# Weights and row buffers moved from 16 to 32 columns (64 to 128 bytes) off the 256-byte lines of the moving operands

## The chip, the cores and the metric

The kernel runs on one core of a Trainium2 chip, all in float32. The metric is the device time of one execution in microseconds (us); three runs of the kernel before took 1356.17, 1356.43 and 1363.1 us. PE is the matrix engine, PEld its weight loads, DVE the vector engine, ACT the scalar engine, POOL and SP the two others.

## The reference, cut to what matters

256 tokens of width 1024 go through two transformer blocks, batch 1, one layer each.

```python
# block 1
h = rmsnorm(x, g1) * (1 + scale1) + shift1
proj = h @ w_in                                  # 1024 x 6976, split into 12 parts
ya = gla(gq, gk, gv, gr, glow) @ w_branch_a      # chunked gated linear attention
yb = sparse_attention(dq, dkv, iq, ik, iw) @ w_branch_b   # 64 keys kept for each query
x = x + gate1 * ((sigmoid(za) * ya + sigmoid(zb) * yb) @ w_out)
h2 = rmsnorm(x, g2) * (1 + scale2) + shift2
q = h2 @ peer_w_q                                # top 16 of 16384 experts, for 8 heads
a = gelu(h2 . u[idx]) * gate                     # 128 rows of u and of v for each token
x = rmsnorm(x + gate2 * sum(a * v[idx]))
# block 2
z = rmsnorm(x) @ w_in_2                          # gates, a 31-tap and a 3-tap causal convolution
x = x + (g_a * (silu(ln(conv(a))) @ w_a_out) + g_b * (s @ w_b_out)) @ w_o
u = rmsnorm(x) @ w_up_2                          # 1024 x 5632
x = x + (gelu(conv(u[:, :2816])) * u[:, 2816:]) @ w_down
x = rmsnorm(x + sigmoid(rmsnorm(x) @ w_ple_gate) * (p @ w_ple))
```

## The kernel before, in words

**Products in three passes.** Activations lie transposed in the on-chip memory: channels on the 128 partitions, the 256 tokens as columns. A float32 weight chunk is split into a high part (ACT copies it to the faster float32 format, line 1310, `hi`) and a low part (DVE subtracts, line 1917, `lo`, written over the raw chunk); the activations are split in the same way. A block of 128 output channels is then the sum over eight slices k of three matmuls, each with its own 128x128 weight load and 256 moving columns:

```python
pe.matmul(out, hi[:, k, c0:c0 + m], x_hi[:, k, 0:n], ...)   # line 754
pe.matmul(out, lo[:, k, c0:c0 + m], x_hi[:, k, 0:n], ...)   # line 755
pe.matmul(out, hi[:, k, c0:c0 + m], x_lo[:, k, 0:n], ...)   # line 756
```

Lines 794 to 796 (token-major products of `gv`, where the activations are the loaded side and the weights the moving one) and 1224 to 1226 (the down product) are the same three passes. A few products run once over whole float32 (line 746).

**Stages, in order of time.** To about 36 us PE forms norms and the first query products. From 36 to 303 us it works through the projections, attentions and output products of block 1, with weights in `ring`. From 303 to 367 us come the expert queries ("pq"), with activations `x2_hi`, `x2_lo` whose rows have 258 columns. From about 385 to 960 us the expert rows are gathered: POOL issues indirect DMAs of 8 KB per partition into 16 row buffers (`rows`, line 661), DVE forms the dot products (line 2335), ACT builds diagonal matrices `diag` (line 1582), and PE adds the scaled rows in plain float32 (line 1090). From 974 us on block 2 runs from 2 MB chunks in three raw slots and three `w_hi` slots; the up and down products take from 1154 to 1337 us. The order of the work on PE is written out by hand; a product waits by semaphores for its chunk and its output bank.

**Places in the partition.** Columns below are float32 columns, 4 bytes. The tensors are laid out by hand in one long stretch; `LINE` is 64 columns (256 bytes). All split activations (`n_hi`, `n_lo`, `g_`, `d_`, `m_`, `c_`, `h_`, `f_`, the first row of `x2_`) begin a whole number of lines from each other, and so does each slice k but in `x2_`, where each row is 258 columns and slice k so lies 2k columns on. The constant `ASIDE` (16 columns) sets the following that many columns past such a line: the ring (`a_ring`, with `e_raw`, `e_hi`, `e_lo`, `w_hi`, `pq_ring`), the raw slots and `w_lo` (`a_raw`), the first `hi` chunk, `pq_row`, the 16 row buffers, `diag`, the expert sums `pacc`, the score buffers `s_all`, and a few buffers behind the raw slots (`sT`, `scb`, `zg`, `scc`, `gelu2`, `otok`). Padding of `LINE - ASIDE` brings what follows back to a line. Chunks and their column blocks inside are whole multiples of 128 columns, so every weight of a three-pass matmul of one kind begins at the same place in its line.

Of the kernel before, what the change touches and what calls it, by code (L numbers as in the profile page):

```python
# [223 lines left out]
def two_blocks(nc, w, out):  # L224
    with ExitStack() as ctx:
# [29 lines left out]
        stat = sb("stat", [P, 2, T])  # L255

        SIZE = 28352
        LINE, ASIDE = 64, 16

        def overlay(*tensors):  # L260

# [2550 lines left out]
```

## Time and profile before

| what | us |
|---|---|
| median of three runs | 1356.43 |
| the profiled execution's own time | 1367.78 |
| its span in the trace | 1366.1 |
| PE busy | 1219.6 |
| PEld busy (overlaps PE) | 913.7 |
| DVE busy | 1065.1 |
| ACT busy | 612.5 |
| POOL busy | 285.8 |

A matmul's busy time runs from its start to its modelled end, and those of neighbours overlap: what a matmul takes of the engine is the distance from its start to the next one's. In a row of groups the mean ns of one is the length from start to end; a window's row counts the matmuls whose busy time touches the window. The idle time before a group is what PE stood still. Times in the trace's views are from the span's start.

### The profile page before, as it was taken

How to read it: one execution, taken by the hardware profiler on the slowest of the kernel's cores; microseconds unless marked ns; L12 is line 12 of the kernel's file. 1: busy time of each engine (PE TensorE's matmuls, PEld its weight loads, DVE VectorE, ACT ScalarE, POOL GpSimd, SP SyncE). 2: the span in 40 equal slices, each digit the busy share in tenths (PEclk: the TensorE clock that was granted, in tenths of full speed). 3: DMA queues.
4: the chain of work that ended last, by engine and by line, in shares of the span. 5: the costliest groups of instructions: out<-in, count | busy, mean ns of one | idle time of the engine just before them, and what ended most of it. 6: DMA issues, size and time to landing. Idle time of an engine off the chain costs nothing. (4 is left out here: it accounts for less than half of the span.)

```text
span 1366.1 us, 19459 instructions
## 1 busy us (share of the span) xinstructions
PE 1219.6 (89%) x6934; PEld 913.7 (67%) x6934; DVE 1065.1 (78%) x2167; ACT 612.5 (45%) x1267; POOL 285.8 (21%) x278
## 2 busy tenths in 40 slices
PE   8999999999997777777877777778999999999998
PEld 6999999999843232322322323223699999999998
DVE  7897678887997777777766777776799968989566
ACT  4666555655433333332333333323652356544345
POOL 1010000003374444434444443442000000000000
PEclk9999999999999999999999999999999999999999
DMA  9966446665999999999999999999744345554461
GB/s 390 375 223 257 175 176 226 246 217 225 353 425 428 427 427 428 427 428 427 426 428 427 427 428 427 428 427 426 286 157 173 130 169 188 179 187 170 165 226 44
DMA packets 55200, 416.64 MB, mean 305 GB/s; under 512 B 6081, under 2 KB 6721, under 8 KB 8658
## 3 DMA queue, kind: packets, MB, share of 16 engines
q0 software_dynamic: 36864, 268.45, 46.8%
q1 hardware_dynamic: 17792, 146.51, 29.1%
q8 instruction: 50, 0.82, 0.2%
q10 hardware_dynamic: 466, 0.63, 0.1%
q14 instruction: 28, 0.23, 0.0%
HBM read 414.52 MB, written 1.05 MB: 304 GB/s over the span
## 5 line engine op out<-in xcount | busy, mean ns | idle before, releaser
L1090 PE MATMUL ps<-arena 128*128 128x512 f32 x512 | 235.2, 603 | 66.0 <-ACT arena L1582 65.7
L1090 PE MATMUL ps<-ring,arena 128*128 128x512 f32 x440 | 210.2, 628 | 45.1 <-ACT arena L1582 44.5
L2335 DVE CUSTOM_DVE_ANT_0 arena<-arena 128x1024 f32<-128x1024 f32 x128 | 151.5, 1222 | 102.6 <-DMA arena<-in_experts,rowid 99.9
L1090 PEld LDWEIGHTS ps<-arena 128*128 128x128 f32 x512 | 92.5, 189 | 205.7 <-ACT arena L1582 110.9
L661 POOL DMA_INDIRECT arena<-in_experts,rowid x128 | 127.4, 996 | 354.1 <-DVE rowid L2262 183.5
L1090 PEld LDWEIGHTS ps<-ring,arena 128*128 128x128 f32 x440 | 85.2, 199 | 167.6 <-issue 91.6
L755 PE MATMUL ps<-h_hi,w_lo 128*128 128x256 f32 x700 | 195.7, 280 | 0.0
L1575 ACT ACTIVATE arena<-arena 128x2 f32<-128x2 f32 x126 | 25.6, 203 | 369.2 <-DVE arena L2335 369.0
L754 PE MATMUL ps<-h_hi,w_hi 128*128 128x256 f32 x672 | 189.5, 282 | 0.6 <-DVE w_lo L1917 0.4
L756 PE MATMUL ps<-h_lo,w_hi 128*128 128x256 f32 x672 | 187.9, 280 | 0.0
L2335 DVE CUSTOM_DVE_ANT_0 ring<-ring,arena 128x1024 f32<-128x1024 f32 x112 | 133.3, 1222 | 30.9 <-DMA ring<-in_experts,rowid 21.3
L661 POOL DMA_INDIRECT ring<-in_experts,rowid x112 | 129.7, 1158 | 130.9 <-PE ps L1090 86.3
L1917 DVE TENSOR_TENSOR w_lo<-arena,w_hi 128x4096 fp32r<-128x4096 f32 (+1 forms) x30 | 122.1, 4068 | 34.2 <-ACT w_hi L1310 33.6
L1310 ACT ACTIVATE w_hi<-arena 128x4096 fp32r<-128x4096 f32 (+1 forms) x30 | 100.2, 3341 | 74.1 <-DMA arena<-in_up_w 29.2
L755 PEld LDWEIGHTS ps<-h_hi,w_lo 128*128 128x128 f32 x700 | 131.7, 188 | 0.2
L754 PEld LDWEIGHTS ps<-h_hi,w_hi 128*128 128x128 f32 x672 | 127.7, 190 | 1.7 <-DVE w_lo L1917 1.3
L756 PEld LDWEIGHTS ps<-h_lo,w_hi 128*128 128x128 f32 x672 | 126.3, 188 | 0.0
L754 PE MATMUL ps<-n_hi,e_hi 128*128 128x256 f32 (+1 forms) x352 | 101.4, 288 | 0.2 <-issue 0.2
L755 PE MATMUL ps<-n_hi,e_lo 128*128 128x256 f32 (+1 forms) x352 | 98.0, 278 | 0.0
L756 PE MATMUL ps<-n_lo,e_hi 128*128 128x256 f32 (+1 forms) x352 | 98.0, 278 | 0.0
L1917 DVE TENSOR_TENSOR e_lo<-ring,e_hi 128x2048 fp32r<-128x2048 f32 (+1 forms) x38 | 86.3, 2271 | 12.5 <-ACT e_hi L1310 11.9
L1582 ACT ACTIVATE arena<-ident,arena 128x128 f32<-128x128 f32 x252 | 85.4, 386 | 0.0
(423 smaller groups left out, 2559.5 us busy)
## 6 DMA issues: line engine op xcount, KB each, us to landing
ring<-in_early_w SPq DMA_DIRECT2D x43, 1024.0 KB, 5.0
arena<-in_ada_w SPq DMA_DIRECT2D x24, 1024.0 KB, 8.7
arena<-in_up_w SPq DMA_DIRECT2D x11, 2048.0 KB, 7.9
arena<-in_z_w SPq DMA_DIRECT2D x8, 2048.0 KB, 8.0
arena<-in_down_w SPq DMA_DIRECT2D x8, 1408.0 KB, 6.0
arena<-in_o_w SPq DMA_DIRECT2D x2, 2048.0 KB, 8.4
arena<-in_early_w SPq DMA_DIRECT2D x3, 1024.0 KB, 6.5
arena<-in_experts,rowid POOLq DMA_INDIRECT x128
```

Of the source, the lines that this page charges most:

```text
L661: pool.indirect_dma_start(out=rows[j], out_offset=None, in_=w["experts"], in_offset=bass.IndirectOffsetOnAxis(ap=rowid[:, even, j:j + 1], ...
L754: pe.matmul(out, hi[:, k, c0:c0 + m], x_hi[:, k, 0:n], start=k == 0, stop=False, skip_group_check=True)
L755: pe.matmul(out, lo[:, k, c0:c0 + m], x_hi[:, k, 0:n], start=False, stop=False, skip_group_check=True)
L756: return pe.matmul(out, hi[:, k, c0:c0 + m], x_lo[:, k, 0:n], start=False, stop=k == KD - 1, skip_group_check=True)
L1090: mm = pe.matmul(BK[4 + 2 * t + b], diag[:, j, :], rows[j][:, D + b * 512:D + (b + 1) * 512], start=first and j == 0, stop=last and j == ( ...
L1310: act.activation(hi, whole, ACT.Copy).then_inc(S("w_hi"), 1)
L1575: act.activation(gel[:, even, two], dots[:, even, two], ACT.Gelu).then_inc(S("act_head"), 1)
L1582: act.activation(diag[:, j, :], ident[:, :], ACT.Copy, scale=amul[:, even, j:j + 1]).then_inc(S("diag"), 1)
L1917: v.tensor_tensor(lo, whole, hi.bitcast(F32), ALU.subtract).then_inc(S("w_lo"), 1)
L2335: v.tensor_tensor_reduce(out=u, in0=u, in1=h2tok[:, t, :], scale=1.0, scalar=0.0, op0=ALU.mult, op1=ALU.add, accum_out=dots[:, even, j:j + ...
```

## The change

One constant of the placement goes from 16 to 32 columns, 64 to 128 bytes:

```diff
         SIZE = 28352
-        LINE, ASIDE = 64, 16
+        LINE, ASIDE = 64, 32
```

Everything named above that stands `ASIDE` past a line moves on by 16 columns; what stands on a line stays where it was, and the total size is the same, since each step aside is paired with padding of `LINE - ASIDE`. No instruction, wait, DMA or size changes, and none changes its order. The distance from moving operand to weights goes from 16 to 32 columns in the three-pass products (for slice k of `x2_` from 16 - 2k to 32 - 2k; for lines 794 to 796, where weights move and activations are loaded, the other way round). `diag` and the row buffers move together, and so do raw chunk, `hi` and `lo`.

## Rows read from the trace of the kernel before

**Rows 1.** The page's first part: busy us, share of the span, instructions.
```profile
PE 1219.6 (89%) x6934; PEld 913.7 (67%) x6934; DVE 1065.1 (78%) x2167; ACT 612.5 (45%) x1267; POOL 285.8 (21%) x278
```

**Rows 2.** The page's second part: granted PE clock in tenths, 40 slices.
```profile
PEclk9999999999999999999999999999999999999999
```

**Rows 3.** Windows: stretch, length, PE, PEld, DVE, ACT, POOL busy, clock, DMA share, GB/s.
```profile
385.00:900.00 515.00, 400.07 (x858) 159.00 (x856) 382.45 (x988) 173.84 (x584) 227.10 (x216) 0.98 1.01 427
...
1020.00:1080.00 60.00, 60.00 (x438) 57.48 (x438) 59.06 (x114) 19.59 (x18) 0.00 (x0) 1.00 0.42 151
...
1200.00:1260.00 60.00, 60.00 (x512) 60.00 (x511) 54.06 (x81) 29.38 (x27) 0.00 (x0) 1.00 0.46 165
```

**Rows 4.** Who waited for whom on PE, 385 to 974 us: us, times, longest.
```profile
PE ps L1090 <- ACT arena L1582: 128.2, 91, 2.5
```

**Rows 5.** The same view, 1158 to 1341 us.
```profile
PE ps L754 <- DVE w_lo L1917: 0.2, 1, 0.2
```

**Rows 6.** The page's costliest groups: busy us, mean ns, idle before.
```profile
L755 PE MATMUL ps<-h_hi,w_lo 128*128 128x256 f32 x700 | 195.7, 280 | 0.0
...
L755 PEld LDWEIGHTS ps<-h_hi,w_lo 128*128 128x128 f32 x700 | 131.7, 188 | 0.2
```

**Rows 7.** Timeline of PE near 1200 us: start, length; nine matmuls.
```profile
1199.74 0.28 PE L755 MATMUL ps<-h_hi,w_lo 128*128 128x256 f32 x1
...
1200.68 0.28 PE L754 MATMUL ps<-h_hi,w_hi 128*128 128x256 f32 x1
```

**Rows 8.** The same near 1343 us; ten matmuls.
```profile
1342.75 0.28 PE L756 MATMUL ps<-h_lo,w_hi 128*128 128x256 f32 x1
...
1343.77 0.28 PE L756 MATMUL ps<-h_lo,w_hi 128*128 128x256 f32 x1
```

**Rows 9.** Groups by shape, 1200 to 1260 us, then 238 to 300 us.
```profile
L754 PE MATMUL ps<-h_hi,w_hi 128*128 128x256 f32 x170 | 47.8, 281 | 0.0
...
L755 PE MATMUL ps<-d_hi,e_lo 128*128 128x256 f32 x64 | 18.0, 281 | 0.0
```

**Rows 10.** Groups by shape: 90 to 100, 106 to 122, 1045 to 1060 us.
```profile
L755 PE MATMUL ps<-n_hi,e_lo 128*128 128x256 f32 x30 | 8.3, 276 | 0.0
...
L795 PE MATMUL ps<-e_lo,n_hi 128*128 128x256 f32 x48 | 13.2, 276 | 0.0
...
L754 PE MATMUL ps<-h_hi,w_hi 128*128 128x256 f32 x45 | 12.4, 276 | 0.0
```

**Rows 11.** Windows of PE alone: stretch, length, busy (count), clock, DMA share, GB/s.
```profile
85.00:103.00 18.00, 18.00 (x162) 1.00 0.57 192
...
236.00:300.00 64.00, 64.00 (x546) 1.00 0.65 236
303.00:333.00 30.00, 30.00 (x253) 1.00 0.49 176
...
1013.00:1033.00 20.00, 20.00 (x172) 1.00 0.55 211
1044.00:1063.00 19.00, 19.00 (x170) 1.00 0.31 111
...
1199.00:1271.00 72.00, 72.00 (x614) 1.00 0.44 160
1273.00:1335.00 62.00, 62.00 (x529) 1.00 0.57 207
```

**Rows 12.** Timeline of PE: a wait at 1158 us, other work at 1341 us.
```profile
1158.12 0.39 PE L754 MATMUL ps<-h_hi,w_hi 128*128 128x256 f32 x1 [0.22 <-DVE w_lo L1917]
...
1340.96 1.03 PE L1205 MATMUL ps<-sq,ones 128*128 128x256 f32 x4
1341.64 0.47 PE L754 MATMUL ps<-h_hi,w_hi 128*128 128x256 f32 x1
```

**Rows 13.** Groups by shape, 303 to 333 us: the 258-column rows.
```profile
L754 PE MATMUL ps<-x_hi,pq_row 128*128 128x258 f32 x48 | 13.9, 289 | 0.0
L755 PE MATMUL ps<-x_hi,pq_row 128*128 128x258 f32 x48 | 13.6, 283 | 0.0
```

**Rows 14.** DMA in 40 slices from 0 to 36 us: GB/s.
```profile
GB/s 0 5 155 355 437 419 428 437 392 437 428 419 437 437 437 391 401 437 437 419 437 437 419 428 391 410 337 428 437 401 419 437 396 423 442 459 410 419 428 410
```

## The prediction

> **What bounds the kernel now.** I read the engines' shares first: PE is busy 89% of the span [rows 1] and its clock is granted at the upper level, 2.4 GHz, nearly throughout [rows 2]. Then the windows, to see which stage has which limit. From 385 to 900 us the DMA engines are full, share 1.01 at 427 GB/s, while PE is busy 400 of 515 us and DVE 382 [rows 3]; PE waits 128 us in all for the diagonals [rows 4], which hang on the gathered rows. In this stage PE's own pace is worth nothing. In the two-block ends it is all: from 1200 to 1260 us PE is busy 60.00 of 60 us beside DVE's 54.06 [rows 3], and in the 183 us from 1158 to 1341 it waited once, for 0.2 us [rows 5]. So a nanosecond more or less per three-pass matmul there is a nanosecond of the kernel's time, until DVE is full.
>
> The reader is next to look at the pace, and the mean length of a group hides it: the costliest such group has 280 ns over 700 matmuls [rows 6]. The starts tell it. Near 1200 us eight steps take 1200.68 - 1199.74 = 0.94 us, 117.5 ns each [rows 7]; near 1343 us nine steps take 1.02 us, 113.3 ns each [rows 8]. Same instructions, same places of both operands, same clock, no wait. The length of a matmul goes with it, 281 ns in the slow rhythm [rows 9] and 276 in the quick one [rows 10], so that a row of groups shows at a glance which rhythm a stretch had. The windows confirm the sizes over many: 614 matmuls in 72 us, less about 2.4 that merely overlap the window's ends (281/117.7), make 117.7 ns; 162 in 18 us, less 2.4, make 112.8, which with the timeline's 113.3 I round to 113.3 [rows 11]. The difference taken is 4.4 ns.
>
> Each rhythm holds once it is there. It changes only where the stream is broken: by plain float32 products, as at 1341 us, after which it was quick, or by a wait, as at 1158 us, after which it stayed slow [rows 12]. Following the lengths through the trace I find slow some 118 us before 303 us (236 to 300 us is the longest piece) and some 249 us after 974 us, of which 183 are the up and down products in one piece; quick some 83 us before 303 (85 to 123 us the longest) and some 77 us after 974 (989 to 1009, 1044 to 1063, 1136 to 1154, 1343 to 1352) [rows 11]. That is 367 us of slow and 160 us of quick rhythm, about 3114 and 1412 matmuls.
>
> **The change part by part.** It adds, removes and moves no instruction, so every term is a change of pace or nothing.
>
> Three-pass products: their weights stand 16 columns from the moving operands' place, and will stand 32. What that does to the pace no row shows, since every such product of before, in both rhythms, has 16. The bounds come from the two rhythms and from one more row. If all slow stretches ran quick: 3114 x 4.4 ns = 13.7 us less (9.3 after 974 us, 4.4 before 303 us). If all quick ones ran slow: 1412 x 4.4 = 6.2 us more. The third row is the expert queries, whose slices stand at 16, 14, ... 2 columns' distance and at starts that aren't multiples of 4 columns: there the pace is neither, since 303 to 333 us hold 253 matmuls of which the 192 of three passes, with lengths of 283 to 289 ns [rows 13], take by the starts about 120.6 ns each. Such a pace everywhere would cost 3114 x 2.9 + 1412 x 7.3 = 19.3 us. So the bounds are -13.7 and +19.3 us.
>
> Which value I take: both rhythms stand at one and the same distance, so it isn't the distance alone that decides but the relative time of load and stream after each break. A new distance shifts the address phase of the two, hence at least throws the dice anew for every stretch. By the breaks of before, rather more than half fall into the slow rhythm (of twenty single blocks between 133 and 230 us 13 were slow; of nine long stretches after 974 us five). With 55% slow, 2490 of 4526 matmuls are slow instead of 3114: 624 x 4.4 = 2.7 us less. The draw is coarse, because the up and down products are one piece: they alone are worth 1550 x 4.4 = 6.8 us.
>
> The Trainium skill speaks against any effect at all. Its page SBUF — State Buffer, section "SBUF: two separate sides", has it that PE has ports of its own and never waits on anyone, and TensorE: Matmul & The Clock Gate, section "What happens when you issue a matmul", that the moving operand and the weight load have independent read ports, so that loading doesn't steal from the running matmul. By that rule the time would stay 1356.4; the two rhythms and the expert queries' 120.6 ns [rows 7, 8, 13] show that the pace of a stream with unchanged work does vary, and in the queries with the operands' places.
>
> Expert queries (303 to 367 us): distances go from 16-2k to 32-2k columns, about 380 matmuls. Taken as unchanged; the bounds are 380 x (113.3 - 120.6) = 2.8 us less and, mirrored, 2.8 us more.
>
> Row buffers: the gathers' landing places move by 64 bytes, from 16 to 32 columns past a line. Buffers on a line itself took 437 GB/s in the slices of the first 36 us [rows 14], those at 16 columns 427 with another kind of DMA [rows 3]. Taken at nothing; the bound is the distance of these two rows, 2.3% of 575 us, 13 us either way, which I hold for very unlikely as 64-byte multiples served both. `diag` and rows move together, so line 1090 keeps its distance, and its pace lies under the DMA anyway [rows 3, 4]. DVE's dot product reads one operand on a line and one aside: if it became slower, DVE has 132 us to spare in 515 [rows 3]. Raw, `hi` and `lo` move together, so lines 1310 and 1917 keep theirs.
>
> If PE gets quicker, DVE is late next: from 1020 to 1080 us it is already busy 59.06 of 60 us [rows 3], so gains there may be lost; 54.06 in 60 would be 54.06 in 57.7 between 1200 and 1260, still under.
>
> The sum: -2.7 us on the profiled execution's 1367.78 (span 1366.1 and 1.7 around it). That execution lies 11.35 us over the median of the runs, and the slow and quick shares of the others aren't shown; I apply the difference to the median: 1356.4 - 2.7 = 1353.7.
>
> **The rivals.**
> Quick everywhere. At 32 columns load and stream no longer meet at a bad phase, and each restart falls into the 113.3 ns rhythm. For it: a quick rhythm exists as a stable one at 16, and both 16 and, with roles exchanged, -16 hold it [rows 10]; 32 is the farthest place in a 64-column line. Against it: nothing shows that the phase counts in 64 columns. Its time: all of 9.3 us after 974, about half of 4.4 before 303, where chains through ACT and DVE also count: 11.5 less, 1344.9.
>
> Slow everywhere: 6.2 more, 1362.6. For it: the slow one already holds two thirds.
>
> A worse rhythm, the rival on the other side. Place: the three-pass stream, most of all 1154 to 1341 us, where nothing covers it [rows 5]. Mechanism: at the new distance the weight load meets the moving stream at a phase that costs more in every matmul, as in the expert queries, 120.6 ns or above. It decides from a mean pace of 118.5 ns: with 4526 matmuls at a mean of 116.4 now, 1.5 ns more is the 6.8 us of half a per cent. At 120.6 the time is 1375.7. Against it: the queries have odd starts in the line too, which the change makes nowhere new.
>
> No effect: the pace depends on the place within 64 bytes or less, and timing is unchanged to the nanosecond: 1356.4. This is what the skill's rule says; for it, that both rhythms occur at one distance.
>
> **How the numbers follow.** Within half a per cent (6.8 us) is what a measurement here can't tell from no change. Dice thrown anew 0.37 (0.09 of it faster, where the long stretch turns quick and little turns slow; 0.27 same; 0.01 slower); quick everywhere 0.24, faster; slow everywhere 0.10 (0.08 same, 0.02 slower); no effect 0.09, same; a worse rhythm 0.20, slower. So faster 0.33, same 0.44, slower 0.23. The likeliest gives 1353.7, its own range 1345 to 1361. Quick everywhere reaches down to 1342.7; of the worse rhythm I take in the nearer half, to 1372: range 1343 to 1372.
>
> **What would show it.** In the trace after: the group lengths by stretch (276, 281, or something else), and starts near 1200 us at 113.3, 117.7 or another distance. Dice: both lengths again, in other stretches. Quick everywhere: 276 throughout and PE idle time before line 754 growing as DVE becomes late. Worse: lengths over 282 in the up products. No effect: the same stretches with the same lengths. The stage from 385 to 960 us should keep its 427 GB/s; if its length changes by over 3 us, my zero for the row buffers was wrong. A third stable pace, or a change in stages without three-pass products, would make the prediction wrong in kind.

## The result, and the profile after

The changed kernel takes 1384.09 us in the median (1382.11 to 1384.97, four runs) against 1358.11 us (1356.17 to 1363.1, four runs) before: 1.0189 times as long, with a 95% interval of 1.0169 to 1.0208. That is 26 us slower, 12 us beyond the slow end of the predicted range. The profiled execution took 1384.97 us, with a span of 1383.2.

The windows of the kernel after, in the stretches of [rows 3] and [rows 11] (columns as in rows 3 for the first two; PE alone, as in rows 11, for the others):

```profile
400.00:900.00 500.00, 379.43 (x814) 148.79 (x813) 367.53 (x955) 166.45 (x555) 204.52 (x204) 0.99 1.01 422
1200.00:1260.00 60.00, 60.00 (x502) 60.00 (x501) 53.62 (x74) 26.57 (x25) 0.00 (x0) 1.00 0.51 186
...
236.00:300.00 64.00, 64.00 (x542) 1.00 0.66 241
...
1199.00:1271.00 72.00, 72.00 (x602) 1.00 0.49 181
```

Two things stand there. From 1199 to 1271 us PE is as full as before and gets through 602 matmuls where it did 614 [rows 11]. And while the expert rows are gathered, the DMA engines are as full as before, share 1.01, and move 422 GB/s where they moved 427 ([rows 3]; from 400 to 900 us it is 427 as well).

The groups by shape from 1200 to 1260 us, and PE's timeline there, two starts that lie fifteen matmuls apart:

```profile
L755 PE MATMUL ps<-h_hi,w_lo 128*128 128x256 f32 x168 | 47.7, 284 | 0.0
L756 PE MATMUL ps<-h_lo,w_hi 128*128 128x256 f32 x167 | 47.6, 285 | 0.0
L754 PE MATMUL ps<-h_hi,w_hi 128*128 128x256 f32 x167 | 46.9, 281 | 0.0
```

```profile
1219.82 0.28 PE L754 MATMUL ps<-h_hi,w_hi 128*128 128x256 f32 x1
...
1221.62 0.28 PE L754 MATMUL ps<-h_hi,w_hi 128*128 128x256 f32 x1
```

The lengths are neither 276 nor 281 ns throughout but 281, 284 and 285 [rows 9, 10], and the starts are 1.80 us / 15 = 120.0 ns apart. By the distances between starts, the trace after has two paces: 120.0 ns from 1170 to 1356 us, from 1053 to 1074 and from 127 to 159, and 118.6 ns nearly everywhere else. The quick rhythm of 113.3 ns is gone.

The page's row of GB/s in 40 slices shows the gathers at the new rate from slice 12 to 28; the granted clock is as in [rows 2]:

```profile
GB/s 388 373 215 238 189 157 234 237 218 230 355 423 420 423 421 422 422 422 421 421 421 421 421 422 422 422 422 422 298 142 170 140 170 177 182 183 164 162 221 36
```

### The profile page after: what moved, and what is told of

It reads as the page before. It is cut to its first block, busy times and chain, and to the rows that moved or that the text cites. A ratio compares the mean times of both kernels' runs of the same rounds, so it can differ in the third digit from the quotient of the medians.

```text
span 1383.2 us, 19459 instructions
## 1 busy us (share of the span) xinstructions
PE 1229.8 (89%) x6934; PEld 922.6 (67%) x6934; DVE 1065.1 (77%) x2167; ACT 612.8 (44%) x1267; POOL 274.8 (20%) x278
## 4 chain that ended last, share of the span: by engine, by line
PE 35%; DMA 30%; DVE 4%; issue 3%; ACT 2%; POOL 1%; DVEq 0%; ACTq 0%; POOLq 0%
DMA ring<-in_experts,rowid 30%; PE ps L1090 7%; PE ps L756 7%; PE ps L755 7%; PE ps L754 6%; PE ps L746 2%; PE ps L1226 2%; PE ps L1225 2%; PE ps L1224 2%; DVE ring L2335 1%; DVE h_rows L2335 1%; PE ps L1179 0%; ACT arena L1578 0%; ACT arena L1582 0%; POOL arena L661 0%
## 5 line engine op out<-in xcount | busy, mean ns | idle before, releaser
L661 POOL DMA_INDIRECT ring<-in_experts,rowid x112 | 118.4, 1057 | 141.3 <-PE ps L1090 103.9
```

The source lines that it names most:

```text
L661: pool.indirect_dma_start(out=rows[j], out_offset=None, in_=w["experts"], in_offset=bass.IndirectOffsetOnAxis(ap=rowid[:, even, j:j + 1], ...
```

## The experiments

The theory formed on this trace, A: two causes that have nothing to do with each other. The pace of the three-pass matmuls follows the **distance** between weights and moving operands in a 256-byte line; the time of a landing packet follows the **absolute place** of its destination. Its rivals: B, the absolute place of the weights decides both; C, the distance decides both. (By the addresses that the build assigns, the arena, which is the kernel's one long stretch, begins 41920 bytes into the partition, 192 past a multiple of 256. So before, weights and row buffers lay on multiples of 256 and after 64 past them. No trace shows this start. Were it another, each "past a multiple of 256" below would be past the place that the row buffers of before have in their line; the steps of 64 bytes between the kernels would stand. DMA records of the gathers' 8 KB packets, between 400 and 880 us and without the few over 340 ns, have a mean of 309.0 ns before, nearly all exactly 309, and of 313.6 after, mostly 312, some 319.)

**Each cause alone.** `e1_base64` keeps the distance and moves the whole layout; `e2_aside128_land0` has the new distance and the old absolute places of weights and row buffers. In both, 64 columns were taken out of a reserve so that the layout still fits.

```diff
-        sb("to_line", [P, 8])
+        sb("to_line", [P, 24])        # e1; e2: [P, 56], and ASIDE = 32
-        SIZE = 28352
+        SIZE = 28288
-        at[0] += LINE - 8 + ASIDE
+        at[0] += ASIDE - 8
```

> Distance of weights and moving operands as before (64 bytes), but the whole layout moved on by 64 bytes, so that weights and row buffers lie at the same absolute places in a 256-byte line as after the change (64 past a multiple of 256). Theory A (two causes: the pace of the three-pass matmuls follows the distance, the landing of DMA packets follows the absolute place): paces of 113.3 and 117.8 ns only, packets of the gathers at 312 to 319 ns as after the change, gather stage some 6.9 us longer than before: about 1365. Theory B (the absolute place of the weights decides both): paces of 118.6 and 120.0 as after, about 1384. Theory C (the distance decides both): as before, 1358.

> Distance of 128 bytes as after the change, but the base moved so that weights and row buffers lie on multiples of 256 bytes, as before. Theory A: paces of 118.6 and 120.0 ns, packets back at 309 ns, gather stage as before: 1384 - 7 = 1377. Theory B: paces of 113.3 and 117.8, all as before: 1358. Theory C: as after, 1384.

The ratio of the kernel after is to the four runs of before beside it (1358.11), the others' to the nine of the first row.

| kernel | distance, place of weights and rows (bytes past 256) | us, median | ratio to before (95%) | paces, ns | gather packets, mean ns |
|---|---|---|---|---|---|
| before | 64, 0 | 1356.99 (9 runs) | | 113.3 and 117.8 | 309.0 |
| after | 128, 64 | 1384.09 | 1.0189 (1.0169 to 1.0208) | 118.6 and 120.0 | 313.6 |
| e1 | 64, 64 | 1365.29 | 1.0059 (1.0042 to 1.0076) | 113.3 and 117.8 | 313.6 |
| e2 | 128, 0 | 1374.71 | 1.0123 (1.0095 to 1.0152) | 118.6 and 120.0 | 309.0 |
| e4 | 0, 192 | 1385.9 | 1.0207 (1.018 to 1.0234) | 120.0 | 313.7 |
| e5 | 192, 128 | 1375.89 | 1.0134 (1.0107 to 1.0161) | 117.8, two short stretches at 113.3 | 313.6 |

Windows of e1, then of e2 (columns as in rows 3):

```profile
400.00:900.00 500.00, 379.40 (x809) 148.43 (x808) 363.66 (x939) 167.52 (x559) 204.10 (x204) 0.98 1.01 422
1200.00:1260.00 60.00, 60.00 (x532) 60.00 (x531) 55.74 (x79) 30.22 (x28) 0.00 (x0) 1.00 0.49 178
```

```profile
400.00:900.00 500.00, 389.10 (x826) 153.89 (x824) 370.42 (x956) 168.78 (x564) 212.75 (x207) 0.97 1.01 427
1200.00:1260.00 60.00, 60.00 (x502) 60.00 (x501) 52.44 (x71) 26.89 (x27) 0.00 (x0) 1.00 0.51 185
```

The reader sees the two marks come apart: e1 has 422 GB/s and 532 matmuls in 60 us, e2 427 GB/s and 502. (The 532 are the quick rhythm, which e1 had in that stretch; the first profile of before had the slow one, 512.) Theory A holds in both, with 1365.3 us for an expected 1365 and 1374.7 for 1377; B and C fall. The pace alone costs 17.7 us (12.9 to 20.6 by the interval of the ratio), the landing 8.3 (5.7 to 10.3), together 26.0. The change cost 26.0 us against its own runs of before and 27.1 against the nine of the table; that the sum agrees to the tenth is luck. The stages agree with the split. Against `e3_before_again` below, e1 is 7.9 us longer from the first scaled row to block 2 and 0.6 us in all the rest; e2 is 4.9 us longer up to the expert queries, 13.0 us in block 2 and under 0.1 us in between.

**Other distances in the kernel.** `e4_aside0` and `e5_aside192` have `ASIDE = 0` and `ASIDE = 48`.

> Distance 0, weights and row buffers at 192 past a multiple of 256. Theory A: the packets of the gathers take 309 only on a multiple of 256 bytes, so 312 to 319 here too (+7 us); should a multiple of 64 off either side differ, it shows here. Pace: if the two reads collide most at equal places, 120 ns or more, at least 1384; if the distance's effect is monotonous (a larger distance is worse), 113.3 throughout and about 1352.

> Distance 192 bytes (that is, -64 in a line of 256), weights and row buffers at 128 past a multiple of 256. If the pace counts in a line of 256 bytes and is symmetric, as lines 794 to 796 suggest (quick at -64 before), 113.3 and 117.8 as before; if not, a pace of its own, 118 or over. Packets: 309 if the landing wants multiples of 128 bytes, 312 to 319 if it wants multiples of 256.

Timeline of e4, then of e5, each with starts fifteen matmuls apart:

```profile
1219.80 0.28 PE L755 MATMUL ps<-h_hi,w_lo 128*128 128x256 f32 x1
...
1221.60 0.28 PE L755 MATMUL ps<-h_hi,w_lo 128*128 128x256 f32 x1
```

```profile
1219.78 0.28 PE L756 MATMUL ps<-h_lo,w_hi 128*128 128x256 f32 x1
...
1221.55 0.28 PE L756 MATMUL ps<-h_lo,w_hi 128*128 128x256 f32 x1
```

120.0 ns at distance 0 and 1.77/15 = 118.0, by the longer stretch 117.8, at 192 bytes, where it is the pace nearly throughout. In two places e5 has the quick one, 276 ns long and 1.70/15 = 113.3 ns apart. The first, 103 to 123 us, is lines 794 to 796, where activations are loaded and weights move, so that the distance counts the other way round. The second is the last block of three passes, in the ordinary roles. The rows are from the groups by shape of 105 to 122 us and from the timeline:

```profile
L794 PE MATMUL ps<-e_hi,n_hi 128*128 128x256 f32 x51 | 14.1, 276 | 0.0
```

```profile
1362.41 0.28 PE L756 MATMUL ps<-h_lo,w_hi 128*128 128x256 f32 x1
...
1364.11 0.28 PE L756 MATMUL ps<-h_lo,w_hi 128*128 128x256 f32 x1
```

So the pace isn't monotonous in the distance: 0 and 128 bytes are the slow ones. And 64 and 192 bytes hold the same two paces, but not equally often: at 64 bytes the quick one has 30% and 64% of the three-pass matmuls in the two profiles of the kernel before, at 192 bytes some 5%. The packets are slow at 64, 128 and 192 bytes alike; only a multiple of 256 was quick.

**The pace by itself.** `m1_pe` has only streams of the three passes on an otherwise idle core.

```python
for at in range(0, 64, 4):          # columns from the moving operands' place to the weights'
    for n in (1, 2, 3, 4):
        breaks(n)                   # n plain float32 matmuls, 256 columns
        stream(at)                  # 72 matmuls: hi*x_hi, lo*x_hi, hi*x_lo
```

> A kernel with nothing of the model: 64 streams of 72 three-pass matmuls (128x128 weights, 256 columns), activations copied from x, on quiet engines, each after 1 to 4 plain float32 matmuls as a break. The distance from moving operand to weights goes from 0 to 60 columns in steps of 4, four streams each. The pace as a function of the distance alone (theory A) gives 120.0 ns at 0, both 113.3 and 117.8 at 16, 118.6 or 120.0 at 32 and 117.8 at 48; steps of 4 columns show whether 16 columns are the grain (flat between) or 4 are. If other engines or DMAs have a part in it, the quiet streams all run at one pace.

Its timeline, pairs of starts thirty matmuls apart, at 0, at 16 after one break matmul, at 16 after two, at 32 after one and at 52 columns:

```profile
37.77 0.28 PE L283 MATMUL ps<-x_hi,w_hi 128*128 128x256 f32 x1
41.37 0.28 PE L283 MATMUL ps<-x_hi,w_hi 128*128 128x256 f32 x1
...
192.77 0.28 PE L284 MATMUL ps<-x_hi,w_lo 128*128 128x256 f32 x1
196.17 0.28 PE L284 MATMUL ps<-x_hi,w_lo 128*128 128x256 f32 x1
...
201.82 0.28 PE L283 MATMUL ps<-x_hi,w_hi 128*128 128x256 f32 x1
205.36 0.28 PE L283 MATMUL ps<-x_hi,w_hi 128*128 128x256 f32 x1
...
343.29 0.29 PE L283 MATMUL ps<-x_hi,w_hi 128*128 128x256 f32 x1
346.89 0.29 PE L283 MATMUL ps<-x_hi,w_hi 128*128 128x256 f32 x1
...
538.78 0.28 PE L285 MATMUL ps<-x_lo,w_hi 128*128 128x256 f32 x1
542.28 0.28 PE L285 MATMUL ps<-x_lo,w_hi 128*128 128x256 f32 x1
```

They make 120.0, 113.3, 118.0, 120.0 and 116.7 ns. Over the second half of each stream:

| columns | ns | columns | ns | columns | ns | columns | ns |
|---|---|---|---|---|---|---|---|
| 0 | 120.0 | 16 | 113.3 or 117.8 | 32 | 118.7 or 120.0 | 48 | 117.8 |
| 4 | 118.2 to 120.0 | 20 | 118.7 | 36 | 118.3 or 120.0 | 52 | 116.7 |
| 8 | 118.3 | 24 | 117.3 or 118.7 | 40 | 119.9 | 56 | 116.7 or 117.8 |
| 12 | 117.7 or 123.5 | 28 | 120.0 | 44 | 118.1 | 60 | 117.3 or 120.1 |

The quiet streams have the paces that the kernels at 0, 16, 32 and 48 columns have, to 0.1 ns. So no other engine and no DMA is needed for them: weight loads and moving streams of PE alone have these paces. By what mechanism isn't shown. Four columns already make a difference, and of the sixteen distances only 16 columns showed 113.3 ns. But four streams don't show every pace of a distance: at 48 columns all four had 117.8, and e5 has 113.3 there too. The Trainium skill's page SBUF — State Buffer, section "SBUF: two separate sides", has it that PE never waits on anyone. As to other engines this run agrees, with the same paces whether they work or not. The skill's page TensorE: Matmul & The Clock Gate, section "What happens when you issue a matmul", has weight load and moving stream use independent ports, so that the load takes nothing from the stream. This run differs: the pace depends on how the two addresses stand to each other, and 0 and 16 columns lie 6.7 ns apart.

**The landing by itself.** `m2_landing` has nothing but 8 plain loads, then 8 gathers, of 1 MB at each place.

> A kernel with nothing of the model: eight loads of 1 MB by SP's queue, then eight gathers of expert rows by POOL's, at each of the places 0, 4, 8, 16, 24, 32, 40, 48, 56, 1 and 0 columns past a multiple of 256 bytes, nothing else running. If the landing place sets a packet's duration: 309 ns at 0, some 313 to 314 at 16, 32 and 48 in the gathers; the plain loads likewise, unless only gathers are sensitive. If contention with the engines' accesses is the cause, 309 everywhere.

Shares of the 8 KB packets at 309 ns or under, and their mean without those over 340, by the DMA records:

| columns past 256 bytes | 0 | 4 | 8 | 16 | 24 | 32 | 40 | 48 | 56 | 1 | 0 again |
|---|---|---|---|---|---|---|---|---|---|---|---|
| loads, share | 0.96 | 0.42 | 0.55 | 0.64 | 0.70 | 0.75 | 0.67 | 0.65 | 0.52 | 0.39 | 0.96 |
| gathers, share | 0.99 | 0.39 | 0.50 | 0.63 | 0.89 | 0.86 | 0.76 | 0.72 | 0.72 | 0.40 | 0.98 |
| gathers, mean ns | 309.05 | 313.1 | 311.9 | 310.8 | 309.7 | 309.9 | 310.3 | 310.5 | 310.7 | 313.1 | 309.25 |

With no engine at work a multiple of 256 is still the one place where nearly every packet takes 309 ns, so the place matters by itself. But at 16 columns the quiet gathers lose 0.6%, the kernel's 1.5% (309.0 to 313.6): the direction is shown, the rest of the size is open. What is different there, more gathers in flight or the engines' accesses to the buffers, wasn't tried. Nor does the place cost the same in every stage: of e1's plain 8 KB loads from 40 to 300 us, at 64 bytes past, 98% take 309 ns or less, as in the kernel before (97%). The DMA engines were busy 0.64 of that time, and 0.97 to 1.01 in the gathers and in m2's loads; whether it is this that matters wasn't tried.

**Which rhythm, and when.** `e3_before_again` is the kernel before once more.

> The kernel before, unchanged, for a second profile. If the rhythm of each stretch is drawn anew in each execution, the stretch from 1158 to 1341 us may be quick (113.3 ns) here and the execution about 7 us shorter than the 1367.78 of the first profile; if it is fixed by the program, every stretch has its rhythm again and the time is 1367 to 1368.

Its windows of PE, the groups by shape from 1200 to 1260 us, and a pair of starts fifteen matmuls apart:

```profile
236.00:300.00 64.00, 64.00 (x547) 1.00 0.66 237
1013.00:1060.00 47.00, 47.00 (x379) 1.00 0.44 150
1199.00:1271.00 72.00, 72.00 (x637) 1.00 0.48 175
```

```profile
L754 PE MATMUL ps<-h_hi,w_hi 128*128 128x256 f32 x178 | 49.1, 276 | 0.0
```

```profile
1219.80 0.28 PE L754 MATMUL ps<-h_hi,w_hi 128*128 128x256 f32 x1
1221.50 0.28 PE L754 MATMUL ps<-h_hi,w_hi 128*128 128x256 f32 x1
```

The time was 1356.59 us, the span 1354.9 against 1366.1. The up and down products, slow in the first profile [rows 9], are quick here: 637 matmuls in 72 us for 614 [rows 11], 276 ns for 281. So one program has its long stretch now at one pace and now at the other. Not every stretch: up to 303 us both profiles of the kernel before and that of e1 have the same pace in every long stretch (quick from 70 to 125 us, slow from 129 to 156 and from 238 to 301). They part only behind the gathers. Counting distances between starts, this execution has 3017 matmuls at the quick pace and 1707 around the slow one; the first profile had 1436 and 3289. Another 3.4 us of the 11.2 are in the expert queries: of the first profile the row for 330 to 345 us is

```profile
330.00:345.00 15.00, 13.07 (x98) 0.89 0.99 400
```

with PE idle for 1.9 of 15 us and, behind the idle time, a stretch at the lower level of 1.2 GHz (a granted clock of 0.89 in the mean); in the second profile the clock was 1.00 there. The idle time is one wait, for ACT's copy of a query (line 1284), by the view of PE's waits:

```profile
PE ps L1047 <- ACT arena L1284: 1.9, 1, 1.9
```

The trace after has the same wait of 1.9 us, and e3, e1 and e2 don't. So it comes with the execution and not with the change. Why ACT was late in these two isn't known.

`m3_breaks` tries what leads into which rhythm at 16 columns.

> A kernel with nothing of the model: 56 streams of 48 three-pass matmuls at a distance of 16 columns, each after a break of another kind: 1 to 8 plain float32 matmuls of 256 columns, 1 to 5 of 128, 1 to 4 of 64, or a wait for ACT of varying length with 0 to 3 matmuls behind it. In the last sweep at 16 columns breaks of 1 and 3 matmuls led into the quick rhythm (113.3 ns) and 2 and 4 into the slow one (117.8). If the number of matmuls in the break decides, odd ones give quick and even ones slow again, whatever the stream before; if the rhythm before or the exact time decides, the same break gives both, and the waits give a mixture.

The parity of the break falls: after two matmuls of 256 columns three streams were quick and two slow, and one matmul gave quick and slow in turn in four streams in a row. But this isn't chance: the rhythm before the break decides with the break. One or two plain matmuls of 256 columns turned the rhythm over each time, three led into the quick one from either, and two of 128 columns kept it. In m1, m3 and `m4_own` (below), 54 streams at 16 columns follow another at 16 columns with only plain matmuls between. They have 26 pairs of a break and a rhythm before it. Sixteen pairs occur more than once, in 44 streams, and none had two outcomes. All six streams right behind a wait for ACT were quick (113.3 ns), all three behind a wait and one matmul slow.

`m4_own` asks whether it is the emptied pipeline:

```python
breaks(n)
if own:
    pe.matmul(BK[7][:, 0:1], ones, ones[:, 0:1]).then_inc(S("own"), 1)
    pe.wait_ge(S("own"), count)
stream(at)
```

> A kernel with nothing of the model: streams of 48 three-pass matmuls after plain float32 matmuls, once directly and once after a wait of PE for its own last matmul. In the sweep of breaks all six streams right behind a wait for ACT ran at 113.3 ns at a distance of 16 columns. If emptying PE's pipeline sets the phase of load and stream, every stream with the own wait is quick at 16 columns, and those without it fall either way (113.3 or 117.8); at the other distances the wait leads to one and the same pace each time (118.7 or 120.0 at 32, 116.7 at 52). If it was the time of ACT's answer, the own wait gives a mixture.

At 16 columns eight of nine streams behind the own wait were quick, and four of nine without it. The slow one had a slow stream before it and a break of one matmul; with a quick stream before it the same break and wait gave quick. At the others it changed little: 118.9 with and 118.5 without at 32, 116.7 both at 52, 120.0 both at 0. So an emptied pipeline favours the quick rhythm, and doesn't guarantee it.

`p1_settle` puts eight such waits into the kernel before:

```diff
+            def settle(key):
+                pe.wait_ge(S("product"), BLOCK_AT[key])
...
+                if b in (6, 10, 14):
+                    settle(("up", b))
                 product_parted(("up", b), h_hi, h_lo)
```

> The kernel before with eight waits of PE for its own preceding block (at ba 2, z 5, 13, 21, 29 and up 6, 10, 14), each some 0.2 us. If an emptied pipeline leads into the quick rhythm at a distance of 16 columns, the stretches behind these waits are at 113.3 ns: 236 to 300 us (2.4 us gained), the stretches of z (up to 2 us), and up and down always quick (nothing to gain where they were quick already, 6.9 us where slow); less 8 x 0.2. About 1353 against 1356.6, and the spread of the runs smaller. If the rhythm is a matter of luck whatever the wait, 1358 with a spread as before.

Its windows of PE, and the timeline around the wait at `ba` 2:

```profile
236.00:300.00 64.00, 63.94 (x563) 1.00 0.66 241
1013.00:1060.00 47.00, 46.94 (x363) 1.00 0.41 141
1199.00:1271.00 72.00, 72.00 (x638) 1.00 0.48 175
```

```profile
239.53 0.28 PE L758 MATMUL ps<-g_hi,e_hi 128*128 128x256 f32 x1
239.64 0.28 PE L759 MATMUL ps<-g_hi,e_lo 128*128 128x256 f32 x1
239.76 0.28 PE L760 MATMUL ps<-g_lo,e_hi 128*128 128x256 f32 x1
240.10 0.39 PE L758 MATMUL ps<-g_hi,e_hi 128*128 128x256 f32 x1
240.32 0.28 PE L759 MATMUL ps<-g_hi,e_lo 128*128 128x256 f32 x1
...
241.48 0.28 PE L760 MATMUL ps<-g_lo,e_hi 128*128 128x256 f32 x1
241.59 0.28 PE L758 MATMUL ps<-g_hi,e_hi 128*128 128x256 f32 x1
241.71 0.28 PE L759 MATMUL ps<-g_hi,e_lo 128*128 128x256 f32 x1
```

1357.54 us in the median of 11 runs, ratio 1.0003 (0.9987 to 1.0019): no gain. The stretch from 236 to 300 us, slow in each other profile at 16 columns (before, e1 and e3), turned quick behind the wait (563 matmuls for 547), some 0.8 us after it, and the up products are quick; but 1013 to 1060 us came out slow (363 for 379), and with the same 16 matmuls fewer took back what the first gained. What did change is the spread: 1356.83 to 1358.22 us in 11 runs, while 15 runs of the kernel before beside it went from 1353.23 to 1364.12. The waits took away the best draws with the worst.

## Why the prediction was wrong

**The pace: the likeliest case was wrong, the rival on the other side came true.** The prediction took the new distance as new dice between the two old rhythms and gave a worse rhythm 0.20. The step that failed is the one from "it isn't the distance alone that decides but the relative time of load and stream" to "throws the dice anew": it kept 113.3 and 117.7 ns as the only likely paces at any distance. Both decide: the distance sets which paces exist, and what went before, the break and the rhythm before it, which of them a stretch takes (m3). A distance of 32 columns has other ones, 118.7 and 120.0 (m1), and e2 shows 17.7 us for that alone, which by itself lies outside the range (1374.71 us). That both rhythms occur at one distance was read as a sign against the distance; it says only that the distance doesn't fix the pace uniquely. What the trace of before held for it was the expert queries, whose distances of 16 - 2k columns ran at neither rhythm [rows 13]; the prediction used them as a bound and not as the nearest row to a distance other than 16, which they were. "Quick everywhere" rested on 32 being the farthest place in the line: m1 has 120.0 ns at 28 and 36 columns too.

**The bound of the worse rhythm was sized on an unusual execution.** 19.3 us came from 3114 slow and 1412 quick matmuls. The medians of the kernel before, 1356.4 to 1358.1 us, are about e3's time, 1356.59, with 1707 and 3017. At 120.6 ns the same sum is 1707 x 2.9 + 3017 x 7.3 = 27 us. That the rival's time, 1375.7, came out near e2's 1374.71 is luck: it set the pace too long (119.26 ns in the mean of e2) and counted too few matmuls as quick, and the two errors cancelled. The prediction said that the shares of the other runs weren't shown and used the profile's all the same; the 11 us between profile and median was their trace: 6.2 us in the up and down products and 3.4 us in the expert queries, by the two traces. From the means of all distances between starts, 119.26 ns in e2 and 115.28 in e3, times 4970 come 19.8 us; 17.7 were measured. That the rest lies in waits is likely and wasn't shown. There is a slip in the rival too: 1.5 ns over a mean of 116.4 is 117.9, not 118.5.

**The landing of the row buffers: taken at nothing, measured 8.3 us** (e1). The bound of 13 us either way held, but was called very unlikely because places on a line and 16 columns aside served alike. The rows compared were of two kinds of DMA and, above all, places relative to the arena: the arena itself begins 192 bytes past a multiple of 256, so that by these addresses "aside" was the aligned place and the line was not. The 437 GB/s of [rows 14] are single slices of 0.9 us, with 337 and 459 beside them; the 36 slices from the fifth on have a mean of 421, so this row couldn't show that the line served as well as the place aside. The fair comparison, one queue at two absolute places, wasn't in the trace of before.

**Right:** the change acts in no other stage. Stage by stage against e3, the trace after loses 5.3 us to the start of the expert queries, 2.1 in them, 7.7 from the first scaled row to block 2, and 13.2 in block 2, of which 9.6 from the first `o` product to the end of the down products. The 2.1 us are the 1.9 us wait for ACT that the first profile of before has too; the queries' own pace stayed, 120.0 ns in the mean before and 119.8 after, as the prediction took it. DVE did not become the bound. And 3 us more in the gather stage was named as the sign that the zero for the row buffers was wrong.

## What to carry to other kernels

Where weight loads and matmuls alternate one to one, take the distances between starts, not the mean length, and test the offset between the two operands within 256 bytes: over steps of 16 bytes the pace here went from 113.3 to 123.5 ns. A place that works once can have a slower rhythm too, so take more than one profile. Work out absolute addresses before calling a place aligned, and where the DMA engines are full, try multiples of 256 bytes as the landing place. When the profiled execution lies 0.8% over the median, find out why before costing anything with its rows.

## What the runs showed of the hardware that wasn't expected

- Three-pass float32 streams have discrete paces that hold for nearly 200 us at a stretch: at 16 columns' distance 113.3 or 117.8 ns per matmul, in one program differently from run to run.
- On a quiet core the pace at 16 columns followed from the plain matmuls of the break and the pace before it: 16 such pairs were met more than once, in 44 streams, never with two outcomes (m1, m3, m4).
- The paces need no other engine: on an idle core they are the same to 0.1 ns (m1).
- At 16 columns a wait for an empty pipeline led into the quick one in 14 of 15 quiet streams (m3 and m4), and in none of three with one plain matmul between wait and stream (m3).
- A gather's 8 KB packet takes 309 ns on a multiple of 256 bytes and 313.6 on average at 64, 128 and 192 past it, in the kernel; on an idle core gathers show the same preference, at 64 bytes less than half as large (309.05 to 310.8), and plain loads show it too (m2); the kernel's plain loads up to 300 us, with the DMA engines busy 0.64 of the time, don't (e1).
